# A second mixer's attention, recurrence and pooling moved between its input units, which are reordered by head

## The reference, cut to what matters

```python
def hybrid_mixer_2(h, w_in, b_f, pool_w, pool_scale, ..., w_out):
    z = h @ w_in
    zp, zq, zk, zv, zf, zx, zy = jnp.split(z, offsets, axis=-1)   # 512, 1024, 1024, 1024, 8, 512, 512 wide
    y_pool = pool_mixer(zp, pool_w, pool_scale)
    y_attn = forgetting_attention(zq, zk, zv, zf, b_f)
    y_lru = rg_lru_branch(zx, zy, ...)
    y = jnp.concatenate([y_pool, y_attn, y_lru], axis=-1)
    return y @ w_out
```

## Time and profile before

| | |
|---|---|
| three runs | 3673.56, 3677.67, 3678.85 us, median 3677.67 |
| the profiled execution | 3672.54 us, its span 3670.8 us |
| TensorE busy | 3388.8 us (92%), mean granted clock 0.965 |
| VectorE busy | 2128.3 us (58%) |
| ScalarE busy | 1157.9 us (32%) |
| moved by DMA | 706.13 MB, mean 192 GB/s |
| `In2`'s 36 units | 2504.6 to 2706.05 us of the span |
| end of the last input unit to the first output unit | 2706.05 to 2797.07 us |

### The profile page before, as it was taken

One profiled execution on the slowest core, in us unless ns is written; L12 is line 12 of the kernel. 1 busy time (PEld: TensorE's weight loads), 2 busy tenths in 40 slices (PEclk: granted clock), 3 DMA queues, 4 the chain that ended last, 5 costly groups with the idle time before them and its releaser, 6 DMA issues. The chain is left out here.

```text
span 3670.8 us, 57947 instructions
## 1 busy us (share of the span) xinstructions
PE 3388.8 (92%) x23176; PEld 2763.7 (75%) x23176; DVE 2128.3 (58%) x3160; ACT 1157.9 (32%) x1456; POOL 166.6 (5%) x277
## 2 busy tenths in 40 slices
PE   6788978989999999988999999998968999999998
PEld 1575466457777799977888888887856788888887
DVE  1082564663332475656777777776465666566566
ACT  1201021032222322234434343434343444344343
POOL 0000000101212100000000000000000000000000
PEclk8899989999999999999999999999988999999999
DMA  8653542732222287743777777773522455555553
GB/s 347 269 206 126 218 161 104 263 127 76 82 68 77 84 349 290 288 170 140 264 272 277 265 278 272 276 262 121 188 103 80 149 183 190 188 184 191 185 181 139
DMA packets 99114, 706.13 MB, mean 192 GB/s; under 512 B 10992, under 2 KB 10992, under 8 KB 17776
## 3 DMA queue, kind: packets, MB, share of 16 engines
q1 hardware_dynamic: 74736, 523.27, 39.4%
q0 software_dynamic: 23184, 169.88, 12.4%
q10 hardware_dynamic: 1008, 10.23, 0.7%
HBM read 697.05 MB, written 6.29 MB: 192 GB/s over the span
## 5 line engine op out<-in xcount | busy, mean ns | idle before, releaser
L2196 PE MATMUL ps<-hT_parts,rows_parts 128*128 128x512 f32 x3300 | 1174.5, 397 | 0.0
L2195 PE MATMUL ps<-hT_parts,ring_parts 128*128 128x256 f32 x3300 | 936.9, 284 | 2.7 <-DVE hT_parts L2146 2.5
L2168 DVE TENSOR_TENSOR ring_parts<-ring,rows_parts 128x2048 fp32r<-128x2048 f32 (+1 forms) x340 | 770.0, 2266 | 248.8 <-ACT rows_parts L2163 247.9
L2163 ACT ACTIVATE rows_parts<-ring 128x2048 fp32r<-128x2048 f32 (+1 forms) x340 | 643.2, 1893 | 459.0 <-DMA ring<-in_mlp_u 217.4
L2196 PEld LDWEIGHTS ps<-hT_parts,rows_parts 128*128 128x128 f32 x3300 | 626.1, 190 | 129.3
L2195 PEld LDWEIGHTS ps<-hT_parts,ring_parts 128*128 128x128 f32 x3300 | 630.3, 191 | 24.8 <-DVE hT_parts L2146 14.3
L2196 PE MATMUL ps<-work_parts,rows_parts 128*128 128x512 f32 x1616 | 574.7, 397 | 0.0
L487 PE MATMUL ps<-hT,ring 128*128 128x256 f32 (+1 forms) x1472 | 462.0, 476 | 24.4 <-ACT work L734 9.7
L2195 PE MATMUL ps<-work_parts,ring_parts 128*128 128x256 f32 x1616 | 453.8, 281 | 0.0
L487 PEld LDWEIGHTS ps<-hT,ring 128*128 128x128 f32 x1472 | 282.0, 192 | 203.6 <-issue 174.3
L2196 PEld LDWEIGHTS ps<-work_parts,rows_parts 128*128 128x128 f32 x1616 | 304.3, 188 | 68.5
(11 more groups left out here) (428 smaller groups left out, 3509.6 us busy)
## 6 DMA issues: line engine op xcount, KB each, us to landing
ring<-in_mlp_u SPq DMA_DIRECT2D x128, 1024.0 KB, 5.0
ring<-in_ffn_u SPq DMA_DIRECT2D x88, 1024.0 KB, 4.8
rows<-in_mod_r POOLq DMA_DIRECT2D x64, 1024.0 KB, 5.2
ring<-in_gate_u SPq DMA_DIRECT2D x64, 1024.0 KB, 5.9
work<-in_ada_r POOLq DMA_DIRECT2D x64, 1024.0 KB, 5.3
ring<-in_in_u SPq DMA_DIRECT2D x36, 1024.0 KB, 4.8
ring<-in_mod_u SPq DMA_DIRECT2D x32, 1024.0 KB, 9.4
rows<-in_ada_r POOLq DMA_DIRECT2D x32, 1024.0 KB, 7.6
```

The lines of the kernel that those rows point to most:

```text
L2163: act.activation(unit_high(u)[:, 0:size], slot(u)[:, 0:size], ACT.Copy).then_inc(hi_done, 1)
L2168: dve.tensor_tensor(ring_parts[:, u % SLOTS, 0:size], slot(u)[:, 0:size], unit_high(u)[:, 0:size].bitcast(F32), ALU.subtract)\
L2195: pe.matmul(ps[:, b, low_half], low, top(kt), start=False, stop=False)
L2196: mm = pe.matmul(ps[:, b, :], high, both(kt), start=False, stop=kt == kts - 1)
```

## The change

The host reorders `in2_u`, the input units, by `IN2_ORDER`: zx, zp, zy, then for each head its q, k and v unit; and the rows of the output matrix to pool, recurrence, attention. `Mix2` is gone as a stage. Its pieces are functions (`Forget`, `Lru`, `Pooled`, `Head`) with the same arithmetic, called between the units of `In2`, whose loop is written out. Units of head h are 12 + 3h to 14 + 3h. The forget products follow unit 1. A head's values are turned on their own and written back over `zv`. Outputs are written over the inputs' tiles (pool over `zp`, recurrence over `zy`, head over `zq`) and split from there in five pieces instead of four, each when its part is ready. Scratch tiles move so that nothing still in use is overwritten; `hT` is no longer used for outputs or values.

```diff
+IN2_ORDER = [*range(28, 32), *range(4), *range(32, 36), *(g + h for h in range(AH) for g in (4, 12, 20))]
+        def split_tiles(dve, own, x, at):
+            n = x.shape[1]
+            own.step(dve.tensor_copy(h_low[:, at:at + n, :], x))
+            own.settle()
+            dve.tensor_tensor(h_high[:, at:at + n, :], x, h_low[:, at:at + n, :].bitcast(F32), ALU.subtract).then_inc(x_split, n)
...
+            ATT.append(dict(v=aux(), l=aux(), t=aux(), o=aux()))
...
+            def vector_decay(dve, own, k):
+                if k == 0:
+                    dve.wait_ge(lru_tanh, 1)
+                    own.step(dve.tensor_scalar(lru_u, lru_t, -1.0, 1.0, ALU.mult, ALU.add))
+                    own.settle()
+                    own.step(dve.reciprocal(lru_u, lru_u))
+                else:
+                    own.settle()
+                    dve.scalar_tensor_tensor(lru_t, lru_t, -2.0, lru_u, ALU.mult, ALU.mult).then_inc(lru_sq, 1)
...
+            def turn(pe, h):
+                use = ATT[h]["t"]
+                pe.wait_ge(pnorm, h + 1)
...
+        class In2:
...
+            def tensor(pe, own):
+                rms_x2.tensor(pe)
+                for n in range(36):
+                    unit_products(pe, seg_in2 + n, in2_use(n), low_then_high(hT_parts), split=2 * KT if n == 0 else None)
+                    h, step = divmod(n - HEAD0, 3)
+                    if n == 1:
+                        forget_products(pe)
+                    if n == 3:
+                        turn_forget(pe)
+                    if n == 9:
+                        Lru.tensor(pe)
+                    if n == 13:
+                        Pooled.tensor(pe)
+                    if h >= 1 and step == 0:
+                        if h >= 2:
+                            Head.weigh(pe, h - 2)
+                        Head.turn_values(pe, h - 1)
+                        Head.logits(pe, h - 1)
+                    if h >= 1 and step == 2:
+                        Head.turn(pe, h - 1)
+                Head.weigh(pe, AH - 2)
+                Head.turn_values(pe, AH - 1)
+                Head.logits(pe, AH - 1)
+                Head.turn(pe, AH - 1)
+                Head.weigh(pe, AH - 1)
+
+            def scalar(act, own):
...
+                for n in range(36):
+                    t = IN2_ORDER[n]
+                    small_out(act, seg_in2 + n, n % 2, u2[:, t:t + 1, :], FIRST, in2_half)
+                    round_unit(act, seg_in2 + n + AHEAD_ACT)
...
+                    if n == 10:
+                        Lru.scalar_gates(act, own)
+                    if n == 13:
+                        Pooled.scalar(act, own)
+                    if n == 14:
+                        Lru.scalar_decay(act)
+                    if n == 19:
+                        Lru.scalar_gelu(act)
+                    if n == 21:
+                        Lru.scalar_root(act)
+                    if h >= 1 and step == 0:
+                        if h >= 2:
+                            Head.out(act, h - 2)
+                        Head.values_out(act, h - 1)
+                        Head.exps(act, own, h - 1)
+                    if h >= 1 and step == 2:
+                        Head.turned_out(act, own, h - 1)
...
+            def vector(dve, own):
...
+                for n in range(36):
+                    t = IN2_ORDER[n]
+                    rest_unit(dve, seg_in2 + n + AHEAD_DVE)
+                    large_add(dve, n + 1, n % 2, u2[:, t:t + 1, :], SECOND, in2_half)
...
+                    if 4 <= n < 8:
+                        Lru.vector_taps(dve, own, n - 4)
...
+                    if 8 <= n < 12:
+                        Pooled.vector(dve, own, n - 8)
+                    if n == 12:
+                        Forget.vector_logs(dve, own)
...
+                    if n in (14, 17, 18):
+                        Lru.vector_gelu(dve, own, (14, 17, 18).index(n))
+                    if n in (19, 20):
+                        Lru.vector_decay(dve, own, n - 19)
+                    if n == 22:
+                        Lru.vector_inputs(dve, own)
+                    if 23 <= n < 27:
+                        Lru.vector_scan(dve, own, n - 23)
+                    if n == 28:
+                        Lru.vector_out(dve, own)
+                    if h >= 1 and step == 0:
+                        Head.maxima(dve, own, h - 1)
+                    if h >= 1 and step == 1:
+                        Head.scaled(dve, own, h - 1)
...
+                evacuated(dve, use_pool[1])
+                split_tiles(dve, own, zp, 0)
+                Head.maxima(dve, own, AH - 1)
+                dve.wait_ge(lru_done, 1)
+                split_tiles(dve, own, zy, 4)
+                Head.scaled(dve, own, AH - 1)
+                for first, last in ((0, 4), (4, 7), (7, 8)):
+                    evacuated(dve, ATT[last - 1]["o"])
+                    split_tiles(dve, own, zq[:, first:last, :], 8 + first)
```

More of the change, by code:

```diff
@@ L2370, in small2 @@
             return smallw2[:, o:o + n]
[L2372 to L2416, removed]
@@ L2476, in tensor @@
                     mm.then_inc(bk.full[use[0]], 1)
[L2478 to L2531, removed]
-                act.activation(fz[1], fz[1], ACT.Exp, scale=-1.0).then_inc(lf_e, 1)
-                act.activation(sp_l[1], sp_l[1], ACT.Exp, scale=-1.0).then_inc(lam_e, 1)
-                act.wait_ge(lf_u, 1)
-                act.activation(fz[3], fz[2], ACT.Ln).then_inc(lf_ln, 1)
-                act.activation(sp_l[3], sp_l[2], ACT.Ln).then_inc(lam_ln, 1)
[L2537 to L2543, removed]
-                    emptied(use, ins)
+            def scalar_gates(act, own):
@@ L2588, in vector, with vector_taps @@
[L2588 to L2593 removed]
+            def vector_taps(dve, own, k):
+                if k == 0:
+                    own.step(dve.tensor_copy(lru_pad[:, :, LRU_TAPS - 1:], zx))
+                    own.settle()
+                for b in range(4):
+                    own.settle(3)
+                    tap = vec("lru_cw", k * 4 + b, k * 4 + b + 1)
+                    src = lru_pad[:, b, k:k + T]
+                    if k == 0:
+                        ins = dve.tensor_scalar(xc[:, b, :], src, tap, vec("lru_cb", b, b + 1), ALU.mult, ALU.add)
+                    else:
+                        ins = dve.scalar_tensor_tensor(xc[:, b, :], src, tap, xc[:, b, :], ALU.mult, ALU.add)
+                    if k == LRU_TAPS - 1:
+                        ins.then_inc(xc_ready, 1)
+                    else:
+                        own.step(ins)
+                own.settle()
@@ new lines, in vector_gates, with vector_gelu @@
+            def vector_gates(dve, own):
+                for n in use_lr:
+                    evacuated(dve, n)
+                for b in range(4):
+                    ins = dve.tensor_scalar(gr[:, b, :], gr[:, b, :], sp_l[3][:, b:b + 1], None, ALU.mult)
+                    if b < 3:
+                        own.step(ins)
+                    else:
+                        ins.then_inc(lru_a, 1)
+            def vector_gelu(dve, own, k):
+                if k == 0:
+                    own.step(dve.tensor_tensor(gi, gi, xc, ALU.mult))
+                    own.step(dve.tensor_tensor(gel, zy, zy, ALU.mult))
+                elif k == 1:
+                    own.settle()
+                    own.step(dve.tensor_tensor(gel, gel, zy, ALU.mult))
+                else:
+                    own.settle()
+                    dve.scalar_tensor_tensor(gel, gel, 0.044715, zy, ALU.mult, ALU.add).then_inc(gelu_in, 1)
@@ L2953, in _ @@
                 In2.scalar(act, own)
-                Mix2.scalar(act, own)
                 Ffn2.scalar(act, own)
```

346 lines of the change are left out of this document (217 added, 129 removed).

## The result

The changed kernel took 3633.51 us (median of four runs, 3628.45 to 3637.88) against 3676.01 (four runs, 3673.56 to 3678.85): 42.5 us less, a ratio of 0.9884 with a 95% interval of 0.9867 to 0.9901. The profiled execution is the slowest of the four, 3637.88 us.

What follows compares the result with a forecast made beforehand. Input units were taken as bound by TensorE, the mixer behind them as a chain of waits. Terms 32.5 + 6.6 + 12.9 + 7.4 = 59.4 against 98.4 gain 39 us: 3637 us, range 3625 to 3657.

Steps and rivals of the forecast that it cites:

- The likeliest case: Whole kernel: the forecast as summed, 3637 us, with its ends 3628 to 3646; chance 0.68.
- TensorE's pieces between units: Between input units: the mixer's matmuls, all in TensorE's queue and so on the path, 32.5 us.
- wait behind unit 20: At turn(1): TensorE waits 3.7 us for normalised rows queued on VectorE behind the decay of unit 19.
- clock lost behind it: Behind the unit 20 wait: slow matmuls cost 2.9 us, as in the first block's MLP, with 0 as other end.
- tail: From the end of unit 35 to output unit 0: 11.9 us plus 1.0 for logits at lower clock, 12.9.
- first output unit: Behind the tail: keeps the 7.43 us that it takes now rather than 5.59, since it follows a like idle.
- The feared 0.1 per block: Some 30 blocks between units: long-met semaphore waits taken at 0; 0.1 each would be 3 us, the upper end.
- The covers: VectorE and ScalarE extras beside input units cost nothing; up to 7.6 us extra on VectorE makes no weight late.
- `turn(2)` behind unit 23: Next candidate for a wait: VectorE's rows done 4.7 us after unit 22 against 5.59, fits by 0.9.
- No stall at unit 20: Rival: lateness at unit 20 is taken up, the 6.6 us term goes, gain 46 us; chance 0.12.
- VectorE's queue late at every head: Rival: six other turns find rows about 1 us late and lose clock, 23 us more, about 3660; chance 0.14.
- Straight code starves TensorE: Rival: instruction fetch waits at the 36 written-out input units lose 63 us, 24 slower, about 3700; chance 0.04.

Runs made afterwards that it cites:

- scaled_first: Changed kernel, but at unit 19 VectorE normalises head 1's rows before the 7.3 us of the recurrence's decay; 3629.24 us, 0.9871 of the kernel before.
- more_at_19: Changed kernel with one more 1024-column reciprocal (6.55 us, unused) at unit 19 between the decay and head 1's normalising; one run, 3643.14 us.
- before_unrolled: Kernel before, with only the loop over the 36 input units written out on TensorE, VectorE and ScalarE; one run, 3680.77 us.
- pieces_behind: Changed kernel with all pieces of forget logs, recurrence, pooling and attention moved behind the 36 input units, in the changed order; one run, 3694.36 us.
- tail: Changed kernel with the last head's chain reordered behind unit 35: logits before weighing head 6, maxima and normalising before splits, exponentials before copies; median 3630.17 us.

## Why the prediction was right, step by step

The forecast was 3637 us with 3625 to 3657 around it; measured were 3633.51 and, again, 3630.00. The likeliest case came, by its own mechanism: one wait behind unit 20, no other up to the tail, and a tail of the order that was written down. Each step against the changed kernel's first profile:

| step | predicted | measured |
|---|---|---|
| TensorE's pieces between units | 32.5 | 29.5 |
| wait behind unit 20 | 3.7 | 3.13 (3.3 with its start) |
| clock lost behind it | 2.9 | 1.6 |
| tail | 12.9 | 14.07 |
| first output unit | 7.4 | 6.84 |
| sum | 59.4 | 55.3 |

**The pieces** were over-priced by 3 us. The stretch of the input units grew from 207.3 to 241.7 us; less 3.3 of wait and 1.6 of clock, 29.5 are left, and the pieces' own rows add up to the same. The block of weigh, value turn and logits took 2.78 where I added 3.04, the turn 0.25 where I took 0.35, the recurrence's products 3.26 for 3.5, the pool's 1.54 for 1.8. The feared 0.1 per block for waits long met was not there. Why the same matmuls start closer here than in the gap was not tried. The prediction's "from 201 to about 240" for the input units looks exact only by chance: 201 misses the start of the first unit, and from the true 207.3 the same terms (32.5 and 6.6) would have given 246.

**The covers** held. No weight and no add came late in 36 units, and the two runs with added reciprocals measure VectorE's: 6.55 us vanish, 13.1 leave a wait of 2.30. The claim that VectorE can be 7.6 us late was even too strict here, because TensorE's pieces (3.0 us of the 10.8) lengthen the two units. This was measured behind unit 29 alone, where no piece stands on VectorE; for the other units, and for ScalarE, there is only the profile without waits.

**The wait behind unit 20** was there, at the place, for the reason (`scaled_first`: it goes; `more_at_19`: it grows one to one), and 0.4 to 0.6 us shorter, since VectorE signalled 8.8 us after the end of unit 19 (2636.23 to 2645.07) and not 9.3. Its clock loss was over-priced by 1.3 us. In the MLP's row matmuls were slow from the first one behind the wait; behind unit 20 the granted clock was 0.87 for the first 1.07 us, then 0.50 until about 2649.5, and full after that. In the MLP another wait of 1.21 us had gone before, a unit earlier; whether that makes the difference was not tried. Over the runs the unit behind a wait took 5.53 us (wait 2.30), 7.17 to 7.26 (3.13) and 7.68 (9.72) where 5.6 is normal. Matmuls at the lower level, 1.2 GHz, are seen behind the two longer ones (granted clock over the unit 1.00, 0.76 and 0.71). `turn(2)` behind unit 23 had 1.5 us to spare (rows ready at 2665.0, wanted at 2666.5).

**The tail** had the order that I wrote, and waits of 6.6 us in all (2.38, 3.50 and 0.70) where I had 6.5; its matmuls at the lower clock level cost 2 us rather than the 1 I took. That is a matter of the run, for where in the tail the clock falls differs: six profiles of the same tail took 11.59 to 14.07 us, so my 12.9 with its 0 to 2 was about as good as can be done.

**The rivals.** "No stall at unit 20" is out by the profile. "VectorE's queue late at every head" is out: no other turn waited. "Straight code starves TensorE" is out by `before_unrolled` and by the absence of issue waits. The rival that I did not have is the one that the experiments brought up: that the order by itself might lose. It does, by 17.5 us in `pieces_behind`, and overlap covers it.

The stretch fell by 43.1 us where I had 39: pieces, wait, clock and first output unit were over-priced by 5.3 us together, and the tail was under-priced by 1.2. That the medians differ by 42.5, so close to 43.1, is partly luck: their noise is as large as this error, and the same two kernels differed by 46.8 the second time.

## What to carry to other kernels

When a stage waits on a chain of small steps and its neighbour keeps one engine busy with long regular units, cut the chain into pieces and put them between the units: the matmuls are paid in full, and the rest was free here as long as the busy engine did not ask for its result before it was due, and VectorE was not late for the units themselves, with two units of slack. Then look for the one long instruction that stands in a queue ahead of something that the busy engine will ask for soon. The wait is the time until that queue has done the long instruction and what is asked for, less the time until it is asked for (here 8.8 less 5.6 us, 3.2), and moving the piece ahead of the instruction removes it. At the end, where no units are left as cover, let the busy engine first do what starts the longest chain elsewhere. The order that is good between units can be a bad one by itself, so such a change can't be judged by trying the order first.

## What was not expected of the hardware

TensorE's loss of clock behind a wait is not in proportion to the wait: none behind 2.30 us, 1.6 us behind 3.13, 2.1 behind 9.72. In `tail` the matmuls of line 2676 took 1.22 us behind waits of 2.29 and 0.70 us, while in `scaled_first`, behind waits of 2.38, 3.50 and 0.70, they took 0.70 and 0.75; the changed kernel's two profiles had tails of 12.41 and 14.07 us. What decides it is open. And code ahead of the change took up to 5.8 us more or less from run to run (the first input unit starts at 2498.2 to 2503.98 us), which is as much as the reordering experiments gain.
